# First layer of a two-layer decoder step: parts of x made from PSUM, residual copied after them, constant products while the first weights are rounded

## The reference, cut to what matters

```python
def rms_normalize(x):
    xf = x.astype(jnp.float32)
    return (xf * lax.rsqrt(jnp.mean(xf * xf, axis=-1, keepdims=True) + EPS)).astype(x.dtype)

def rms_norm(x, g):
    return rms_normalize(x) * g.astype(x.dtype)
...
    xn = rms_norm(hp, norm_mix_even[e])
    (qa, ka, va), (qb, kb, vb) = split_even(xn, w_in_even[e])   # xn @ w_in_even, 1024 x 3072
```

## Time and profile before

| | |
|---|---|
| three runs, median (lowest, highest) | 1647.23 us (1644.51, 1650.3) |
| the profiled execution: its own time | 1648.96 us |
| the profiled execution: span from first to last instruction | 1646.8 us |
| PE busy | 1585.1 us, 96% of the span |
| DVE busy | 525.8 us, 32% |
| ACT busy | 394.5 us, 24% |
| mean granted TensorE clock | 0.981 of full |

### The profile page before, as it was taken

One profiled execution on the slowest core, in us unless ns is written; L12 is line 12 of the kernel. 1 busy time (PEld: TensorE's weight loads), 2 busy tenths in 40 slices (PEclk: granted clock), 3 DMA queues, 4 the chain that ended last, 5 costly groups with the idle time before them and its releaser, 6 DMA issues.

```text
span 1646.8 us, 37458 instructions
## 1 busy us (share of the span) xinstructions
PE 1585.1 (96%) x16845; PEld 1212.8 (74%) x16845; DVE 525.8 (32%) x741; ACT 394.5 (24%) x658; POOL 44.0 (3%) x50
## 2 busy tenths in 40 slices
PE   8989999999999978799999999999999999999997
PEld 7976699999999966594375574676867777768556
DVE  5466554443367665745110101100101011001013
ACT  4236443433347566522000000000000000000001
POOL 0000000000000000000000000000000000000000
PEclk9999999999999998899999999999999999999999
DMA  9566535543434435338989999999999999999996
GB/s 348 180 222 195 154 100 166 178 171 128 154 108 163 166 119 132 93 130 353 419 341 395 416 407 411 416 404 417 414 404 417 402 416 416 403 417 415 406 415 234
DMA packets 143464, 479.46 MB, mean 291 GB/s; under 512 B 31160, under 2 KB 60608, under 8 KB 128723
## 3 DMA queue, kind: packets, MB, share of 16 engines
q1 hardware_dynamic: 140380, 469.08, 74.3%
q0 software_dynamic: 2064, 5.66, 0.9%
q10 hardware_dynamic: 871, 2.42, 0.4%
HBM read 463.56 MB, written 13.55 MB: 290 GB/s over the span
## 4 chain that ended last, share of the span: by engine, by line
PE 54%; DVE 0%; ACT 0%; issue 0%; DVEq 0%
PE ps L2863 35%; PE ps L2879 18%; PE ps L2928 0%; PE ps L2907 0%; PE ps L229 0%; PE ps L2888 0%; PE ps L2913 0%; PE ps L2895 0%; DVE act L3087 0%; DVE act L3077 0%; DVE tail_rows L3077 0%; DVEq L2756 0%; ACT xn_tokens L3143 0%; PE ps L2917 0%; ACT item_y L3128 0%
## 5 line engine op out<-in xcount | busy, mean ns | idle before, releaser
L2863 PE MATMUL ps<-up_ring,item_x 128*32 128x448 f32 x6000 | 566.8, 539 | 0.0
L2863 PEld LDWEIGHTS ps<-up_ring,item_x 128*32 128x32 f32 x6000 | 320.5, 110 | 240.4 <-issue 148.8
L2879 PE MATMUL ps<-down_ring,hid_t 128*32 128x256 f32 x5376 | 298.7, 379 | 1.0
L2879 PEld LDWEIGHTS ps<-down_ring,hid_t 128*32 128x32 f32 x5376 | 244.1, 110 | 55.7 <-issue 10.7
L3049 DVE TENSOR_TENSOR hid<-hid,ps 128x1344 f32<-128x1344 f32 x16 | 24.9, 1555 | 660.3 <-PE ps L2863 658.9
L3128 ACT COPY item_y<-ps 128x512 f32<-128x512 f32 x8 | 4.7, 587 | 429.2 <-PE ps L2879 429.2
L1586 PE MATMUL ps<-x_hi_up,w_hi_up 128*128 128x288 f32 x320 | 86.3, 295 | 0.1
L1587 PE MATMUL ps<-x_lo_up,w_hi_up 128*128 128x288 f32 x320 | 86.3, 297 | 0.0
L3124 ACT ACTIVATE hid<-ps 128x1344 f32<-128x1344 f32 x16 | 20.7, 1292 | 268.6 <-PE ps L2863 246.5
L554 PE MATMUL ps<-x_hi_in_odd,w_hi_in_odd 128*128 128x288 f32 x256 | 70.6, 300 | 0.0
L555 PE MATMUL ps<-x_lo_in_odd,w_hi_in_odd 128*128 128x288 f32 x256 | 70.3, 300 | 0.0
(11 more groups left out here) (524 smaller groups left out, 2013.9 us busy)
## 6 DMA issues: line engine op xcount, KB each, us to landing
up_ring<-in_we_dram SPq DMA_DIRECT2D x250, 896.0 KB, 7.5
down_ring<-in_we_dram SPq DMA_DIRECT2D x112, 1024.0 KB, 10.3
ring<-in_w_ffn_dram SPq DMA_DIRECT2D x23, 1024.0 KB, 6.1
ring<-in_w_in_odd_dram SPq DMA_DIRECT2D x9, 2048.0 KB, 8.1
ring<-in_w_in_even_dram SPq DMA_DIRECT2D x5, 2048.0 KB, 14.4
ring<-in_w_ffn_dram SPq DMA_DIRECT2D x5, 2048.0 KB, 7.8
ring<-in_w_out_odd_dram SPq DMA_DIRECT2D x3, 2048.0 KB, 8.1
odd_layer<-in_we_dram SPq DMA_DIRECT2D x6, 896.0 KB, 12.6
```

Source lines behind the costliest of these rows:

```text
L2863: mm = pe.matmul(k.ps[32 * q:32 * q + 32, 3 * w + g, 0:FW], xg[:, c, g, :], block_of[:, q, :], start=c == 0, stop=c == DC - 1, skip_group_ ...
L2879: mm = pe.matmul(k.ps[32 * q:32 * q + 32, 6 + g // 2, 256 * (g % 2):256 * (g % 2) + 256], hidT[:, 2 * r + j, g, :], block_of[:, j, 256 * q ...
```

## The change

In the first step alone:

- x is turned into six PSUM banks (2 to 7) instead of four; chunks 6 and 7 use the banks of chunks 0 and 1 again, after `copied` and `rest` of those.
- ScalarE makes the high part of each chunk, and VectorE the rest, straight from the PSUM bank. ScalarE copies nothing any more.
- VectorE makes all eight copies to `residual`: chunks 0 and 1 between the first parts, chunks 2 to 7 after `take_lo(dve, 0)` and ahead of `fold`.
- ScalarE waits for all eight copies ahead of `square`; TensorE waits for them ahead of output chunk 2.
- After the transposes TensorE runs `k.warm(pe, 1, 6)`.
- `sum` of the norm comes after output chunk 3, not after output chunk 2.

```diff
 class LateNorm
-    def round_chunk(self, act, c):
-        act.mul(self.parts[0][:, c, :], self.k.residual[:, c, :], self.gain(c)).then_inc(*self.rounded.up())
+    def round_chunk(self, act, c, x):
+        act.mul(self.parts[0][:, c, :], x, self.gain(c)).then_inc(*self.rounded.up())
-    def take_chunk(self, dve, c):
+    def take_chunk(self, dve, c, x):
         dve.wait_ge(*self.rounded.at(c + 1))
...
 stage_load_qkv
+        bank_of = lambda c: 2 + c % 6
...
                 def turn(c):
-                    if c >= 4:
-                        pe.wait_ge(*copied.at(c - 3))
+                    if c >= 6:
+                        pe.wait_ge(*copied.at(c - 5))
+                        pe.wait_ge(*norm.rest.at(c - 5))
                     for i, (a, n) in enumerate(TILES):
-                        mm = pe.transpose(k.ps[:, 4 + c % 4, a:a + n], tok[0:n, i, P * c:P * c + P], ident[0:n, 0:n])
+                        mm = pe.transpose(k.ps[:, bank_of(c), a:a + n], tok[0:n, i, P * c:P * c + P], ident[0:n, 0:n])
...
                 for c in range(4, DC):
                     turn(c)
+                k.warm(pe, 1, 6)
+                pe.wait_ge(*vec_ready.at(2))
...
+                    if m == 2:
+                        pe.wait_ge(*copied.at(DC))
                     if m == SUM:
                         pe.wait_ge(*norm.mean.at(1))
...
-                    if m == 2:
+                    if m == 3:
                         norm.sum(pe, SUM)
...
-                def take(c):
-                    act.wait_ge(*turned.at(c + 1))
-                    act.copy(k.residual[:, c, :], k.ps[:, 4 + c % 4, 0:T]).then_inc(*copied_late.up())
-                    act.wait_ge(*copied_late.at(c - 3))
...
-                for c in range(4):
-                    act.wait_ge(*copied.at(c + 1))
-                    norm.round_chunk(act, c)
-                for c in range(4, DC):
-                    take(c)
-                    norm.round_chunk(act, c)
+                for c in range(DC):
+                    act.wait_ge(*turned.at(c + 1))
+                    norm.round_chunk(act, c, k.ps[:, bank_of(c), 0:T])
...
                 sp_.round_hi(act, 1)
+                act.wait_ge(*copied.at(DC))
                 norm.square(act)
...
-                for c in range(4):
-                    dve.wait_ge(*turned.at(c + 1))
-                    dve.tensor_copy(k.residual[:, c, :], k.ps[:, 4 + c, 0:T]).then_inc(*copied.up())
-                    if c:
-                        norm.take_chunk(dve, c - 1)
-                for c in range(3, DC):
-                    norm.take_chunk(dve, c)
+                def keep(c):
+                    dve.wait_ge(*norm.rounded.at(c + 1))
+                    dve.tensor_copy(k.residual[:, c, :], k.ps[:, bank_of(c), 0:T]).then_inc(*copied.up())
+
+                for c in range(DC):
+                    if c < 2:
+                        keep(c)
+                    norm.take_chunk(dve, c, k.ps[:, bank_of(c), 0:T])
                 sp_.take_lo(dve, 0)
+                for c in range(2, DC):
+                    keep(c)
                 norm.fold(dve)
                 sp_.take_lo(dve, 1)
```

More of the change, by code:

```diff
@@ L364, in gain @@
         return self.k.vec[:, self.first + c:self.first + c + 1]
-    def round_chunk(self, act, c):
-        act.mul(self.parts[0][:, c, :], self.k.residual[:, c, :], self.gain(c)).then_inc(*self.rounded.up())
-    def take_chunk(self, dve, c):
+    def round_chunk(self, act, c, x):
+        act.mul(self.parts[0][:, c, :], x, self.gain(c)).then_inc(*self.rounded.up())
+    def take_chunk(self, dve, c, x):
         dve.wait_ge(*self.rounded.at(c + 1))
-        dve.scalar_tensor_tensor(self.parts[1][:, c, :], self.k.residual[:, c, :], self.gain(c), self.parts[0][:, c, :].bitcast(F32),
+        dve.scalar_tensor_tensor(self.parts[1][:, c, :], x, self.gain(c), self.parts[0][:, c, :].bitcast(F32),
                                  ALU.mult, ALU.subtract).then_inc(*self.rest.up())
@@ L865, in stage_load_qkv @@
         const_in, vec_in, x_in, x_late, second_in = (k.count(n) for n in ("const_in", "vec_in", "x_in", "rows_in", "late_in"))
-        turned, copied, copied_late, vec_ready = k.count("turned"), k.count("copied"), k.count("copied_odd"), k.count("first_ready")
+        turned, copied, vec_ready = k.count("turned"), k.count("copied"), k.count("first_ready")
+        bank_of = lambda c: 2 + c % 6
         done, out = k.count("product_done"), k.count("odd_out")
@@ L904, in _ @@
                 for _ in range(WARM):
-                    pe.matmul(k.ps[:, 3, 0:T], k.ones_wide[:, 0:P], k.ones_wide[:, :], start=True, stop=True)
+                    pe.matmul(k.ps[:, 1, 0:T], k.ones_wide[:, 0:P], k.ones_wide[:, :], start=True, stop=True)
                 pe.wait_ge(*const_in.at(16))
@@ L908, in _ @@
                 pe.wait_ge(*vec_in.at(16))
-                pe.transpose(k.ps[:, 2, 0:NVEC], rows[0:NVEC, :], ident[0:NVEC, 0:NVEC]).then_inc(*vec_ready.up())
+                pe.transpose(k.ps[:, 0, 0:NVEC], rows[0:NVEC, :], ident[0:NVEC, 0:NVEC]).then_inc(*vec_ready.up())
                 pe.wait_ge(*x_in.at(32))
@@ L973, in _ @@
                 dve.wait_ge(*vec_ready.at(1))
-                dve.tensor_copy(k.vec[:, :], k.ps[:, 2, 0:NVEC]).then_inc(*vec_ready.up())
+                dve.tensor_copy(k.vec[:, :], k.ps[:, 0, 0:NVEC]).then_inc(*vec_ready.up())
                 dve.wait_ge(*vec_ready.at(2))
-                for c in range(4):
-                    dve.wait_ge(*turned.at(c + 1))
-                    dve.tensor_copy(k.residual[:, c, :], k.ps[:, 4 + c, 0:T]).then_inc(*copied.up())
-                    if c:
-                        norm.take_chunk(dve, c - 1)
-                for c in range(3, DC):
-                    norm.take_chunk(dve, c)
+                def keep(c):
[5 more added lines that the diff above has]
+                    norm.take_chunk(dve, c, k.ps[:, bank_of(c), 0:T])
                 sp_.take_lo(dve, 0)
+                for c in range(2, DC):
+                    keep(c)
                 norm.fold(dve)
```

## The result

| | before | after |
|---|---|---|
| runs, median (lowest to highest) | 1646.04 us (1641.0 to 1650.58), 20 runs | 1651.34 us (1648.69 to 1654.1), 20 runs |
| the profiled execution: its own time, span | 1648.96, 1646.8 us | 1648.69, 1646.5 us |

The ratio of after to before is 1.0031, with a 95% interval of 1.0023 to 1.0039: the change costs 5.3 us. Yet the two profiled spans are 0.3 us apart, the other way round. A span of one execution can't tell 5 us of 1650, as the spread within each kernel shows; the stretch that the change touches can be compared row by row, and there the loss is plain.

What follows compares the result with a forecast made beforehand. TensorE, busy for 96% of the span, was taken as the bound, through the start of output chunk 4. Moved sum 2.8 plus two clock falls of 1.7 gave +6.2 us on 1647.2, so 1653.4 us; range 1648.6 to 1657.0.

Steps and rivals of the forecast that it cites:

- The bound: TensorE's steady stream: the start of output chunk 4, 31.39 us before, decides, and a shift there reaches the end in full.
- The front: Work up to chunk 2's `hi` phase: piece 0 at 12.05, real products from 14.4, TensorE through over 3 us sooner.
- The first gap: Ahead of chunk 2's `lo` phase: TensorE stands 3.0 us, from 23.0 to 25.95, for the rest of half 1.
- The lead of 0.9 us: Kernel before, chunk 2's `lo` phase: it started at 26.36, while the rest of half 1 was ready at 25.50.
- The moved sum: Sum behind chunk 3: mean at 30.9 instead of 28.12, chunk 4 at 34.2, 2.8 us later, after a second gap.
- The clock: Behind each of the two new TensorE gaps the granted clock falls to 0.50, charged 1.7 us each.
- the case with one fall: Rival, chance 0.22: the clock falls once, not twice, around the two gaps; 2.8 + 1.7 = +4.5 us, 1651.7.
- the forecast of two falls: Main case, chance 0.44: the clock falls behind both gaps; +6.2 us, median 1653.4.
- Not slower: Rival, chance 0.12: rest of half 1 ready by 23.0, no first gap, chunk 4 at 31.2; 1647.0 to 1648.7 us.
- The rival of a clock that is already down when the constant products run: Part of the one-fall rival (0.22): constants end at 17.3, 64 products at 25.9, the first gap is gone; +4.5 us.
- The rule on transposes: Turning of x, 7.03 to 11.53: transposes don't bring about the full clock as matmuls do; the trace doesn't contradict it.

Runs made afterwards that it cites:

- rest_first: The changed kernel with the norm's sum behind chunk 2 again and, on VectorE, the rest of half 1 ahead of the fold; ratio to before 0.9988.
- before_steady: The kernel before with six products of ones at the start instead of five, three on each side of the turned vector table; ratio to before 1.0002.
- sum_back: The changed kernel with the norm's sum behind output chunk 2 again; ratio to before 1.0002.
- before_sum_late: The kernel before with the norm's sum moved behind output chunk 3, nothing else; ratio to before 1.0026.
- no_constants: The changed kernel without its six constant products after the transposes; ratio to before 1.0036.
- rest_only: The changed kernel with the rest of half 1 ahead of the fold on VectorE, the sum staying behind chunk 3; ratio to before 1.0008.

## Why the prediction was right, point by point

- **The number.** The median came out at 1651.34 us, 2.1 below the forecast of 1653.4. Of this, 1.2 is no matter of the change: the kernel before measures 1646.04 in twenty runs, and the forecast stood on 1647.23 from three. The other 0.9 is the sum, +5.3 instead of +6.2. The forecast also put what can be told from no change at 0.3%, 4.9 us; twenty runs of each tell it to 0.08% either way.
- **The bound.** That the start of chunk 4 sets the time held through the variants with one exception: at 30.3 to 31.4 the ratio is 1.000 to 1.001, at 34 to 36 it is 1.0025 to 1.0036, and around 28 it is 0.998 to 0.9995. The exception is `rest_first`, with 32.57 and 0.9988, whose profile caught the early fall. It isn't a ruler for less than a microsecond or two.
- **The front.** Predicted and measured: piece 0 at 12.05 and 12.05; first real product 14.4 and 14.18; rest of half 0 from 14.3 and 14.26; six copies from 16.5 to 18.8 and 16.46 to 18.73; squares from 18.8 and 18.77; rest of half 1 done at 25.9 and 25.86. Rounding from PSUM, which had no row, is hidden by the turning, as it was argued. The landing of half 1 was taken at 14.0 and was 15.0 in this profile; its rounding had 1.8 us to spare, so nothing came of it.
- **The first gap.** 3.0 us predicted, 2.86 measured, with the releaser named. The lead of 0.9 us that the prediction gave TensorE over this chain in the kernel before was right for its profile, and is 0.1 in `before_steady`; the sum doesn't use it.
- **The moved sum.** 2.8 us and a gap of 3.3 were predicted; the gap is 3.29, and the two kernels that isolate the sum confirm it from both sides.
- **The clock.** This term was the largest guess, and by the traces it was set too high. The forecast charged 1.7 us behind each gap. The profile of the change has one fall, worth 1.6. Of the seven gaps of 2.7 to 3.3 us in the profiles (`sum_back`, `before_sum_late`, `no_constants`, `rest_only` and the change), four are followed by a fall. Charging each gap with four sevenths of 1.6 gives an estimate of 2.8 + 1.8 = +4.6. The runs can't settle it: +5.3 lies between the case with one fall (+4.5) and that with two (+6.2), and the interval of the ratio, +3.8 to +6.4 us, holds both. That the forecast of two falls came within 1 us is in part luck.
- **The rivals.** "Not slower", with the rest of half 1 in time, was right as a mechanism: when an edit puts it there (`rest_only`), chunk 4 starts at 31.21, for the predicted 31.2. The change as it stood was 2.9 us from that case, the length of its first gap. The rival of a clock that is already down when the constant products run happens in some executions: in `rest_first` twelve of them took 5.87 us.
- **The rule on transposes.** That the clock fell within gapless transposes, in `rest_first` at 8.6 us, is a row that the profile before didn't have; it was 0.50 from 8.7 to 13.3 with TensorE busy for all of 4.60 us. By the rule in the Trainium skill, page TensorE: Matmul & The Clock Gate, Part 4, transposes don't bring about the full clock as matmuls do. The trace of `rest_first` agrees. In twelve of the fourteen profiles the clock stayed at 1.00 through the same transposes, so they don't always bring it down.

## What to carry to other kernels

A small reduction that feeds a late factor belongs ahead of the last independent work that can cover its way through the other engines. Here two matmuls stood one output chunk too far back, the root and the rounding behind it came 3.2 us later, and TensorE stood for 3.3 us. Where two chains are within a microsecond of each other, speeding up one shows the other: write down both, step by step, and move the work between their steps (here the rest of half 1 ahead of the fold, and two copies to the engine that waits for a load) along with the gain. And where single spans scatter by 5 us, compare the stretch that was changed, and leave the verdict to repeated runs.

## What was not expected of the hardware

- The granted clock can fall in the first 10 us while transposes run without a gap (two of fourteen profiles). It makes the turning of x 6.15 and 6.30 us long instead of 4.50. What this costs depends on what follows: in `rest_first` constant products follow at once, and the first real product came 4.7 us late; in `before_sum_late` it came at 15.49, 0.2 us later than before, and as the clock was also back sooner (by 19 instead of 21), chunk 2's `lo` phase started 0.6 us sooner.
- Where the fall comes within an idle stretch differs too: 2.5 us after the last transpose in the profile before, 0.9 us after it in `before_steady`, with 3.75 and 3.74 us of idling. In `no_constants` it came within an idle stretch of 1.19 us. The sooner fall was the cheaper one here: it was at 0.50 for 6.7 us in both, but TensorE was busy for 5.52 us of them before (14.1 to 20.8) and for 3.85 in `before_steady`.
- A gap of 3.29 us on TensorE was followed by a stretch at 0.50 in two profiles of four with the same gap (`rest_only`, `no_constants`) and not in the two others (the change, `before_sum_late`); one of 2.70 us (`sum_back`) was not, one of 2.86 (the change) and one of 3.01 (`no_constants`) were. The gap's length alone doesn't decide.
- The two chips differ late in the kernel. From the first product of the expert block to the end it is 893.3 us in the four profiles of the chip on which before had 1647.89 us, and 885.8 to 887.0 in the eight of the chip with 1641.1. Within one chip, most of the scatter between these profiles arises ahead of the expert block.
